# Rounding a weight slab at the end of a unit instead of after the chain steps that follow it

## The chip, the cores and the metric

The kernel runs on one core of a Trainium2 chip. A core has five engines that run side by side, each through its own list of instructions in order: PE (TensorE, matrix products), DVE (VectorE), ACT (ScalarE), POOL (GpSimd) and SP (SyncE, which here only issues DMAs). Engines wait for each other by semaphores. Matrix products land in PSUM, which has eight banks; everything else lies in SBUF. The metric is the device time of one execution in microseconds (us), lower is better; with more than one run the median is taken.

## The reference

The input `x` has 256 tokens of 1024 features, in fp32. It goes through two layers.

- **First block.** An adaLN modulation (`silu(c) @ ada_w`, giving shift, scale and gate) of an rms norm, one product with `w_in`, then two branches: an RWKV-7 scan of 8 heads, and attention of 8 heads over a latent of 128 features, in which an indexer scores all keys (`relu(qi . ki)`, weighted by `wi`), the 64 best keys of each query are kept, and a T5 bias is added. Each branch is multiplied by `silu(z)` and by its output matrix (`w_pa`, `w_pb`); the sum, gated by two sigmoids (`g_a`, `g_b`), goes through `w_o`, times the modulation's gate, back onto `x`; then an rms norm.
- **Second block.** A SwiGLU feed-forward part (2816 hidden features), a mixer of two branches (an HGRN2 scan and causal attention with forget gates, "fox"; each with its output matrix, gated, then `w_out`), cross attention to 256 memory tokens, and a second feed-forward part.

```python
br_a = (y_a * jax.nn.silu(z_a)) @ w_pa[l]
br_b = (y_b * jax.nn.silu(z_b)) @ w_pb[l]
merged = jax.nn.sigmoid(g_a) * br_a + jax.nn.sigmoid(g_b) * br_b
x = x + gate[:, None, :] * (merged @ w_o[l])
...
x = x + 0.5 * rmsnorm(swiglu(h, ffn1_w_in[l], ffn1_w_down[l]), ffn1_post_g[l])
```

All of the weights are fp32 and are read once, some 195 MB in all with what is written. The result has to be as precise as fp32 products.

## The kernel before

**Products in three passes.** PE's fast format, fp32r, has fewer bits than fp32. So every operand is split in two: a part rounded to fp32r, and the remainder. A product is three matmuls, hi x hi, hi x lo and lo x hi (`mm3`, L699 to L702). The left or right operand, an activation such as `hThi` and `hTlo`, is split once; the weights are split slab by slab as they come in.

**Slabs.** The weights come as 332 slabs, nearly all of 1024 elements in each of 128 partitions (512 KB). 324 of them are split. Each passes through this line:

1. SP loads it into one of four buffers `raw` (`slab_in`, L647 to L656). The load of slab i waits until slab i-4 is used up: its remainder made, or, if it is a slab that isn't split, PE past it.
2. ACT rounds it: `whi<-raw`, 128x1024, into one of three buffers (`round_slabs`, L1311 to L1321). It waits until the raw slab has landed, and until PE has used the slab three before in the ring (`use`).
3. POOL subtracts: `wlo<-raw,whi` (`remainders`, L2642 to L2656), in four pieces of 128x256, or in one piece in most of the feed-forward parts. It waits for the rounding.
4. PE waits for both (`weights`, L707) and runs the unit's matmuls.

The eight slabs of the modulation's gate (`ada_w`) are not split. PE reads them straight out of `raw` (`gate_unit`, L769; in the trace `ps<-raw,cs`). Two of them follow each of the four groups `g0` to `g3`, the products for the branch gates.

**The order.** Every engine walks the same list, made once in `Plan.lay_out` (L397 to L460) from a table of costs. Its entries are mainly *units*, a slab's product in two halves, and *steps* of *chains*: the serial parts, such as the RWKV heads (`head0`, `head1`), the attention of the first block (`dsa`), the HGRN scan (`hgrn`), the norm at a part's start. Each chain is a generator on each engine, and a step advances it on all of them. Steps stand where the planner thinks that their inputs are ready, between units or halves of units. An engine that has nothing to do in an entry passes on.

**ACT's own list.** ACT's loop (L1818 on) calls `unit(u, half)`. At half 0 it rounds ahead, up to the slab two behind the unit's own (`u.ahead` is three, in the first units two): the buffer for that one was used by the unit just before. At the last half it evacuates finished banks (`outs`, such as `gab`, the branch gates). Between these calls it does the chains' work: `rl` (L1645) copies the indexer's scores out of two banks, with the relu; `x<-ps` copies a head's output; `sq` and `mu` are a head's norm; `olT` (L1657) copies an attention head's output, from which PE makes `ps<-olT,wuv` two heads at a time (L1133); `oahi<-qb` is the rounded half of the fox output's split, and DVE makes its remainder `oalo<-qb,oahi`; `hi_` and `gt` are squares for the mixer's norms. `w2a` is the buffer that takes the modulation gate's sum.

**Banks.** Of the eight PSUM banks the units have three (0 to 2), and the chains five (3 to 7), in turn (`bank`, L693). The first matmul into a bank waits until the engine that had to empty it has done so.

Of the kernel before, what the change touches and what calls it, by code (L numbers as in the profile page):

```python
# [470 lines left out]
def program(nc, I, consts, vecs, out):  # L471
    with ExitStack() as ctx:
# [6 lines left out]
        slabs, place, order = plan.slabs, plan.place, plan.order  # L479
# [824 lines left out]
        def scalar(e):  # L1304
# [3 lines left out]
            def act(o, i, f, **k):  # L1308
                return e.activation(o, i, f, **k)  # L1309

            def round_slabs(upto):  # L1311

                while ahead[0] < min(upto, len(plan.split)):
                    c = ahead[0]
                    i = plan.split[c]
                    n = slabs[i][1][0] * slabs[i][1][1]
                    w.wait_ge(S["raw", i % NRAW], i)
                    if c >= NHL:
                        w.wait_ge(S["mm"], ("use", plan.split[c - NHL]))
                    act(whi[c % NHL][:, 0:n], raw[i % NRAW][:, 0:n], ACT.Copy).then_inc(S["hi"].tick(i), 1)  # L1320
                    ahead[0] += 1  # L1321
# [75 lines left out]
            def post(stage, t):  # L1397
                half = stage in ("f1", "f2")
                r = st[:, 12 + t:13 + t]
                for key in {"f1": [("d1", t, 0), ("d1", t, 1)], "f2": [("d2", t, 0), ("d2", t, 1)],  # L1400
                            "mix": [("wout0", t), ("wout1", t)], "mem": [("wmo0", t), ("wmo1", t)]}[stage]:
                    w.wait_ge(S["ev_a"], key)
                act(r, st[:, 8 + 2 * t:9 + 2 * t], ACT.Identity, bias=st[:, 9 + 2 * t:10 + 2 * t]).then_inc(S["post_a"].tick(), 1)
                w.wait_ge(S["post_a"])
                act(r, r, ACT.Sqrt, scale=(4.0 if half else 1.0) / 1024, bias=C("eps", 2 if half else 0, 1)).then_inc(
                    S["post_a"].tick((stage, t)), 1)
# [57 lines left out]
            def square_out(p, key, t, n):  # L1464
                w.wait_ge(S["ev_v"], key)
                act(p, p, ACT.Square, accum_out=st[:, 8 + 2 * t + n:9 + 2 * t + n]).then_inc(S["ev_a"].tick(key), 1)
# [23 lines left out]
            def unit(u, half):  # L1490
                if half == 0 and u.kind != "gate":
                    round_slabs(place[u.slab] + u.ahead)
                if u.kind == "tail" or (u.kind == "down" and u.last):
                    for n in (range(2) if u.kind == "down" else [half % 2]):
                        t = half if u.kind == "down" else half // 2
                        w.wait_ge(S["mm"], ("acc", u.grp, t, n))
                        square_out(PS[bank_of[u.grp, t, n]][:, :], (u.grp, t, n), t, n)
                        if n == 1:
                            post("f" + u.arg[0], t)
                elif u.last and u.ev in outs and u.kind != "down":  # L1500
                    if u.kind == "tm":
                        w.wait_ge(S["mm"], ("acc", u.grp, half))
                        outs[u.ev](u, half)
                    elif half == 1:
                        w.wait_ge(S["mm"], ("acc", u.grp))
                        outs[u.ev](u, half)

            def turn_over(tag, u):
                b = PS[bank_of["turn", tag, u]]
                w.wait_ge(S["turn_pe"], (tag, u))  # L1510
                act(FF[tag]["a"][0][:, 2 * u:2 * u + 2, :], b[:, :].rearrange("p (j t) -> p j t", j=2), ACT.Copy).then_inc(
                    S["turn_a"].tick((tag, u)), 1)
# [305 lines left out]
            for what, *d in order:  # L1818
                if what == "unit":
                    unit(*d)  # L1820
                elif what == "step":
                    if d[0] in chains:
# [862 lines left out]
        for count in (sync, tensor, vector, scalar, gpsimd):  # L2685
            count(Blank())
        for signal in S.values():
            signal.counted()
        with nc.Block() as block:
            block.sync(sync)  # L2690
            block.tensor(tensor)
            block.vector(vector)
            block.scalar(scalar)
            block.gpsimd(gpsimd)
# [34 lines left out]
```

## Time and profile before

| | us |
|---|---|
| median of 3 runs | 1231.42 |
| lowest and highest run | 1228.05, 1234.56 |
| the profiled execution | 1229.5 |
| its span (first to last instruction) | 1227.7 |

| engine | busy us | share | instructions |
|---|---|---|---|
| PE | 1155.5 | 94% | 8388 |
| POOL | 916.2 | 75% | 927 |
| ACT | 594.4 | 48% | 867 |
| DVE | 466.1 | 38% | 802 |

The mean clock that TensorE was granted is 0.989 of full speed. "Busy" counts each engine's own instructions, whoever waits for them; an engine can be busy for little of the time and still be what others wait for at a given place. The page also lists idle time before a group of instructions and what ended it. That idle time costs something only where the engine that waits is the one that others are waiting for.

### The profile page before, as it was taken

The numbers are of one execution on the slowest core, as the hardware profiler recorded it, in microseconds if no ns is written. First come the engines' busy times: TensorE is split into PE (matmuls) and PEld (weight loads), VectorE is DVE, ScalarE is ACT, GpSimd is POOL, SyncE is SP. The second block draws the span as 40 slices with busy tenths as digits, with TensorE's granted clock in tenths as the row PEclk, the third lists the DMA queues.
The fourth block names the chain that finished last, engine by engine and source line by source line (L and its number), as shares of the span: only waits on it lengthen the run. The fifth ranks groups of instructions, "written<-read, shape, count | busy, mean of one in ns | idle before, by whom it ended". The sixth has DMA issues, their size and how long they took to land.

```text
span 1227.7 us, 21194 instructions
## 1 busy us (share of the span) xinstructions
PE 1155.5 (94%) x8388; PEld 978.1 (80%) x8388; DVE 466.1 (38%) x802; ACT 594.4 (48%) x867; POOL 916.2 (75%) x927
## 2 busy tenths in 40 slices
PE   7999799999899999999999989999899989999997
PEld 7899798677687888788987876878677977888785
DVE  5527555654544111102435566433434133111101
ACT  6374432433656445435554545755345446445433
POOL 4689854531298888796899998678898857888794
PEclk9999999999999999999999999999999999999999
DMA  9887432333165656565565544354675525656562
GB/s 337 269 275 214 121 88 88 103 107 102 65 217 168 201 178 186 169 200 161 144 169 145 145 139 138 105 155 150 197 252 172 155 85 161 198 177 186 169 198 94
DMA packets 182899, 202.10 MB, mean 165 GB/s; under 512 B 7529, under 2 KB 141073, under 8 KB 182033
## 3 DMA queue, kind: packets, MB, share of 16 engines
q1 hardware_dynamic: 177584, 185.78, 50.8%
q10 hardware_dynamic: 5216, 14.97, 3.5%
q8 instruction: 67, 1.10, 0.4%
q14 instruction: 32, 0.25, 0.1%
HBM read 196.51 MB, written 4.21 MB: 163 GB/s over the span
## 4 chain that ended last, share of the span: by engine, by line
PE 67%; POOL 15%; issue 7%; DVE 6%; ACT 4%; POOLq 0%; DMA 0%; ACTq 0%; DVEq 0%
PE ps L700 19%; PE ps L702 18%; PE ps L701 17%; POOL wlo L2654 15%; PE ps L697 11%; PE ps L705 2%; ACT whi L1309 1%; DVE x L1882 1%; DVE oalo L1874 1%; ACT L1309 0%; DVE red L2327 0%; ACT rl L1309 0%; DVE tmp L1879 0%; DVE hE L1874 0%; DVE gt L1874 0%
## 5 line engine op out<-in xcount | busy, mean ns | idle before, releaser
L2654 POOL TENSOR_TENSOR wlo<-raw,whi 128x256 fp32r<-128x256 f32 (+1 forms) x918 | 910.7, 1026 | 294.7 <-ACT whi L1309 293.3
L1309 ACT ACTIVATE whi<-raw 128x1024 fp32r<-128x1024 f32 x324 | 340.3, 1056 | 297.4 <-PE ps L702 267.0
L700 PE MATMUL ps<-whi,hThi 128*128 128x512 f32 (+1 forms) x656 | 264.5, 403 | 14.4 <-POOL wlo L2654 8.9
L702 PE MATMUL ps<-whi,hTlo 128*128 128x512 f32 (+1 forms) x656 | 255.9, 390 | 0.0
L701 PE MATMUL ps<-wlo,hThi 128*128 128x512 f32 (+1 forms) x656 | 255.4, 389 | 0.0
L700 PE MATMUL ps<-hThi,whi 128*128 128x256 f32 x568 | 166.6, 293 | 13.5 <-issue 4.1
L701 PE MATMUL ps<-hTlo,whi 128*128 128x256 f32 x568 | 161.3, 284 | 0.0
L702 PE MATMUL ps<-hThi,wlo 128*128 128x256 f32 x568 | 161.1, 284 | 0.0
L700 PEld LDWEIGHTS ps<-whi,hThi 128*128 128x128 f32 x656 | 123.9, 189 | 46.5 <-issue 18.6
L702 PEld LDWEIGHTS ps<-whi,hTlo 128*128 128x128 f32 x656 | 124.0, 189 | 26.5
L701 PEld LDWEIGHTS ps<-wlo,hThi 128*128 128x128 f32 x656 | 124.2, 189 | 21.9
L700 PEld LDWEIGHTS ps<-hThi,whi 128*128 128x128 f32 x568 | 109.3, 192 | 21.0 <-issue 12.4
L701 PEld LDWEIGHTS ps<-hTlo,whi 128*128 128x128 f32 x568 | 109.5, 193 | 0.1
L702 PEld LDWEIGHTS ps<-hThi,wlo 128*128 128x128 f32 x568 | 109.3, 193 | 0.0
L700 PE MATMUL ps<-whi,aThi 128*128 128x512 f32 x176 | 69.1, 392 | 2.6 <-POOL wlo L2654 2.3
L701 PE MATMUL ps<-wlo,aThi 128*128 128x512 f32 x176 | 68.5, 389 | 0.0
L702 PE MATMUL ps<-whi,aTlo 128*128 128x512 f32 x176 | 68.5, 389 | 0.0
L1874 DVE TENSOR_TENSOR aTlo<-ps,aThi 128x512 fp32r<-128x512 f32 x22 | 15.2, 692 | 111.9 <-ACT aThi L1309 111.9
L1882 DVE SCALAR_TENSOR_TENSOR ac<-ps,st,sg 128x256 f32<-128x256 f32 x44 | 21.1, 484 | 92.5 <-ACT sg L1309 92.5
L700 PE MATMUL ps<-whi,oahi 128*128 128x512 f32 x128 | 52.7, 411 | 3.8 <-DVE oalo L1874 3.1
L1309 ACT ACT_TABLE_LOAD x39 | 50.0, 1283 | 6.5 <-DVE gt L1874 2.6
L701 PE MATMUL ps<-wlo,oahi 128*128 128x512 f32 x128 | 50.7, 396 | 0.0
(386 smaller groups left out, 1538.7 us busy)
## 6 DMA issues: line engine op xcount, KB each, us to landing
raw<-in_w_in SPq DMA_DIRECT2D x120, 512.0 KB, 3.6
raw<-in_ffn_w_in SPq DMA_DIRECT2D x176, 256.0 KB, 3.1
raw<-in_ffn_w_down SPq DMA_DIRECT2D x44, 512.0 KB, 4.2
raw<-in_w_mkv SPq DMA_DIRECT2D x16, 512.0 KB, 6.4
raw<-in_ada_w SPq DMA_DIRECT2D x8, 512.0 KB, 5.6
raw<-in_w_o SPq DMA_DIRECT2D x8, 512.0 KB, 4.3
raw<-in_w_branch_a SPq DMA_DIRECT2D x8, 512.0 KB, 3.7
raw<-in_w_branch_b SPq DMA_DIRECT2D x8, 512.0 KB, 3.7
```

The source lines that it names most:

```text
L697: return e.matmul(o, l, r, start=start, stop=stop)
L700: e.matmul(o, l[0], r[0], start=start, stop=False)
L701: e.matmul(o, l[0], r[1], start=False, stop=False)
L702: return e.matmul(o, l[1], r[0], start=False, stop=stop)
L705: return e.transpose(b[:, o:o + 128], src, ident)
L1309: return e.activation(o, i, f, **k)
L1874: return e.tensor_tensor(o, a, b, op)
L1882: return e.scalar_tensor_tensor(out=o, in0=a, scalar=s, in1=b, op0=op0, op1=op1)
L2654: p = e.tensor_tensor(wlo[c % NHL][:, o], raw[i % NRAW][:, o], whi[c % NHL][:, o], ALU.subtract)
```

## The change

At the end of a unit's second half, behind the evacuation of its banks, ACT now rounds one slab more than it has at this place before: the one three behind the unit's own, whose buffer this very unit has used. Before, this rounding was issued at the start of the next unit, behind all chain steps, table loads, copies and DMA issues that stand between the two. The modulation gate's units, the last ones (`tail`) and the memory keys' (`key`) are left as they are. No instruction is added or removed; on PE, DVE, POOL and SP the order is the same.

```diff
@@ -1504,6 +1504,8 @@
                     elif half == 1:
                         w.wait_ge(S["mm"], ("acc", u.grp))
                         outs[u.ev](u, half)
+                if half == 1 and u.kind not in ("gate", "tail") and u.ev != "key":
+                    round_slabs(place[u.slab] + 1 + u.ahead)
 
             def turn_over(tag, u):
                 b = PS[bank_of["turn", tag, u]]
```

**ACT at the branch gates.** ACT's rows behind the last bank of group `g0` at about 219 us, before. `gab` evacuates the gates' bank, `whi0<-raw3` is the rounding of the third slab of group `g1`.

```order
L1309 ACTIVATE gab<-ps2 128x512
L1309 ACTIVATE rl<-ps7 128x512
L1309 ACTIVATE rl<-ps3 128x512
L1309 ACTIVATE x<-ps4 128x64
L1309 ACTIVATE x<-ps5 128x64
L1309 ACTIVATE sq<-x 128x256
L1309 ACTIVATE x<-ps7 128x64
L1309 ACTIVATE x<-ps3 128x64
L1309 ACT_TABLE_LOAD
L1309 ACTIVATE mu<-mu,con 128x4
L1309 ACTIVATE sq<-x 128x256
L1309 ACTIVATE w2a2<-ps0 128x256
```

The rounding is the next row behind these. The same place after the change:

```order
L1309 ACTIVATE gab<-ps2 128x512
L1309 ACTIVATE whi0<-raw3 128x1024
L1309 ACTIVATE rl<-ps7 128x512
L1309 ACTIVATE rl<-ps3 128x512
L1309 ACTIVATE x<-ps4 128x64
L1309 ACTIVATE x<-ps5 128x64
L1309 ACTIVATE sq<-x 128x256
```

The rounding has moved ahead of eleven rows, the two `rl` copies first. PE's rows at that place, which the change leaves as they are (`raw3,cs` is the modulation gate's slab, in the same buffer `raw3` that the rounding above will read once it is loaded anew; `XU`, `TB`, `TK` belong to a head):

```order
L697 MATMUL ps6<-XU,WT 64x64
L697 MATMUL ps6<-XU,WG 64x64
L697 MATMUL ps0<-raw3,cs 32x256 x4
L697 MATMUL ps7<-XU,TB 64x64 [waits s_ds_a,s_h1_v]
L697 MATMUL ps7<-XU,TB 64x64
L697 MATMUL ps7<-VT,TK 64x64 x2
L697 MATMUL ps3<-XU,TB 64x64 x2
```

The wait for `s_ds_a` in the fourth row is the one for ACT's `rl` copies out of banks 7 and 3.

**ACT at the end of the attention branch**, at about 329 us, before; `whi0<-raw1` is the rounding of the third slab of `w_pa`.

```order
L1309 ACT_TABLE_LOAD
L1309 ACTIVATE gab<-ps1 128x512
L1309 ACTIVATE gab<-ps2 128x512
L1309 ACTIVATE olT<-ps4 128x256
L1309 ACTIVATE w2a2<-ps0 128x256
L1309 ACTIVATE olT<-ps7 128x256
L1309 ACTIVATE whi0<-raw1 128x1024
L1309 ACTIVATE olT<-ps3 128x256
```

And after:

```order
L1309 ACT_TABLE_LOAD
L1309 ACTIVATE gab<-ps1 128x512
L1309 ACTIVATE gab<-ps2 128x512
L1309 ACTIVATE whi0<-raw1 128x1024
L1309 ACTIVATE olT<-ps4 128x256
L1309 ACTIVATE w2a2<-ps0 128x256
L1309 ACTIVATE olT<-ps7 128x256
L1309 ACTIVATE olT<-ps3 128x256
```

Two `olT` copies and a `w2a` copy now stand behind the rounding.

**ACT at the fox output's split**, at about 869 us, before:

```order
L1309 ACTIVATE whi1<-raw1 128x1024
L1309 ACTIVATE oahi<-qb 128x512
L1309 ACTIVATE whi2<-raw2 128x1024
L1309 ACTIVATE oahi<-qb 128x512
L1309 ACTIVATE whi0<-raw3 128x1024
L1309 ACTIVATE oahi<-qb 128x512 x2
```

And after:

```order
L1309 ACTIVATE whi1<-raw1 128x1024
L1309 ACTIVATE whi2<-raw2 128x1024
L1309 ACTIVATE oahi<-qb 128x512
L1309 ACTIVATE whi0<-raw3 128x1024
L1309 ACTIVATE oahi<-qb 128x512
L1309 ACTIVATE whi1<-raw0 128x1024
L1309 ACTIVATE oahi<-qb 128x512 x2
```

Each copy comes one rounding later, and the rounding of `raw0`, which stood behind a DMA issue after the last copy, is now ahead of the last two.

## Rows read from the trace of the kernel before

**Rows 1.** The page: busy time, and two groups of instructions (columns as headed).

```profile
span 1227.7 us, 21194 instructions
...
PE 1155.5 (94%) x8388; PEld 978.1 (80%) x8388; DVE 466.1 (38%) x802; ACT 594.4 (48%) x867; POOL 916.2 (75%) x927
...
## 5 line engine op out<-in xcount | busy, mean ns | idle before, releaser
L2654 POOL TENSOR_TENSOR wlo<-raw,whi 128x256 fp32r<-128x256 f32 (+1 forms) x918 | 910.7, 1026 | 294.7 <-ACT whi L1309 293.3
L1309 ACT ACTIVATE whi<-raw 128x1024 fp32r<-128x1024 f32 x324 | 340.3, 1056 | 297.4 <-PE ps L702 267.0
```

**Rows 2.** The page: the chain that ended last, by engine.

```profile
PE 67%; POOL 15%; issue 7%; DVE 6%; ACT 4%; POOLq 0%; DMA 0%; ACTq 0%; DVEq 0%
```

**Rows 3.** Waits, whole span: us in total, times, longest.

```profile
PE ps L700 <- POOL wlo L2654: 17.4, 17, 2.4
```

**Rows 4.** Waits of PE from 150 to 1212 us.

```profile
PE ps L700 <- POOL wlo L2654: 10.0, 12, 2.4
```

**Rows 5.** Timeline, ACT, 218 to 229 us: start, us, instruction, idle before.

```profile
221.17 1.08 ACT L1309 ACTIVATE rl<-ps 128x512 f32<-128x512 f32 x2 [2.01 <-PE ps L697]
...
228.77 1.05 ACT L1309 ACTIVATE whi<-raw 128x1024 fp32r<-128x1024 f32 x1
```

**Rows 6.** Timeline, SP's issues and ACT's rounding, 223 to 237 us.

```profile
223.51 0.37 SPq L656 DMA_DIRECT2D raw<-in_w_in  x1
...
233.15 0.37 SPq L656 DMA_DIRECT2D raw<-in_w_in  x1
...
236.78 1.06 ACT L1309 ACTIVATE whi<-raw 128x1024 fp32r<-128x1024 f32 x1 [3.58 <-DMA raw<-in_w_in]
```

**Rows 7.** Timeline, PE, 222 to 234 us.

```profile
222.81 0.64 PE L697 MATMUL ps<-raw,cs 128*32 128x256 f32 x8
223.38 0.34 PE L697 MATMUL ps<-XU,TB 128*64 128x64 f32 x4
...
233.27 0.47 PE L700 MATMUL ps<-whi,hThi 128*128 128x512 f32 x1 [2.43 <-POOL wlo L2654]
```

**Rows 8.** Windows: busy time by engine, granted clock, DMA share, GB/s.

```profile
core 0: us, PE busy (x) PEld busy (x) DVE busy (x) ACT busy (x) POOL busy (x), PEclk, DMA share, GB/s
233.20:238.00 4.80, 4.73 (x16) 3.22 (x17) 3.02 (x9) 1.06 (x2) 2.95 (x5) 0.64 0.53 141
...
650.00:750.00 100.00, 91.05 (x1274) 80.16 (x1260) 63.65 (x79) 47.09 (x51) 95.93 (x107) 1.00 0.53 142
880.00:888.00 8.00, 7.28 (x24) 5.60 (x24) 3.58 (x6) 2.08 (x2) 2.85 (x6) 0.79 0.66 216
```

**Rows 9.** Timeline, ACT and PE, 330 to 336 us.

```profile
330.42 0.39 ACT L1309 ACTIVATE olT<-ps 128x256 f32<-128x256 f32 x1
331.06 0.38 ACT L1309 ACTIVATE w2a<-ps 128x256 f32<-128x256 f32 x1 [0.26 <-PE ps L697]
331.88 0.38 ACT L1309 ACTIVATE olT<-ps 128x256 f32<-128x256 f32 x1 [0.44 <-PE ps L697]
334.31 1.06 ACT L1309 ACTIVATE whi<-raw 128x1024 fp32r<-128x1024 f32 x1 [2.04 <-DMA raw<-in_w_pa]
...
333.82 0.65 PE L697 MATMUL ps<-olT,wuv 128*64 128x256 f32 x4
```

**Rows 10.** Timeline, ACT: start of the mixer (576, 586), memory output (1002).

```profile
576.25 1.04 ACT L1309 ACTIVATE hi_<-x 128x1024 f32<-128x1024 f32 x1
...
586.79 2.01 ACT L1309 ACTIVATE whi<-raw 128x1024 fp32r<-128x1024 f32 x2
...
1002.48 1.99 ACT L1309 ACTIVATE whi<-raw 128x1024 fp32r<-128x1024 f32 x2
```

**Rows 11.** Timeline, DVE, POOL and PE, 865 to 885 us.

```profile
870.98 10.20 DVE L1874 TENSOR_TENSOR oalo<-qb,oahi 128x512 fp32r<-128x512 f32 x2 [3.74 <-ACT oahi L1309]
...
882.30 1.28 DVE L1874 TENSOR_TENSOR oalo<-qb,oahi 128x512 fp32r<-128x512 f32 x2
...
865.41 14.62 POOL L2654 TENSOR_TENSOR wlo<-raw,whi 128x256 fp32r<-128x256 f32 x21
...
880.72 0.47 PE L700 MATMUL ps<-whi,oahi 128*128 128x512 f32 x1 [3.06 <-DVE oalo L1874]
```

**Rows 12.** Groups of POOL's instructions, 650 to 750 us.

```profile
L2654 POOL TENSOR_TENSOR wlo<-raw,whi 128x256 fp32r<-128x256 f32 x107 | 96.6, 940 | 4.1 <-ACT whi L1309 4.0
```

## The prediction

> **What bounds the kernel now.** I read the page from the top, then the waits over the whole span, then the places where the change moves something, each in time order. The page shows TensorE (PE) busy 94% of the span, GpSimd (POOL) 75%, ScalarE (ACT) 48% [rows 1]; the chain of waits gives PE 67%, POOL 15%, ACT 4% [rows 2]. So PE sets the time, and POOL where it is late with a remainder `wlo`. POOL waits for ACT's rounded slab `whi` 293.3 us in all [rows 1], but that costs only where PE waits too: PE waits for `wlo` 17.4 us in 17 places [rows 3], of which 10.0 us in 12 places lie behind 150 us [rows 4]. The first number is the reader's trap: almost all of it is slack. An ACT queue that is half idle is not harmless either. ACT runs its list in order, so what a rounding waits for, everything behind it waits for as well. The question is thus not whether ACT has the time, but what stands behind each moved rounding, and whether that rounding can start.
>
> A rounding needs two things: the buffer used three slabs before, which the change waits for at just the right moment, and the raw slab landed. SP loads raw slab i only when slab i-4 is used up (L647-656). Normally that slab's remainder is done long before. Not so at the adaLN gate: its slabs go unsplit into PE (`ps<-raw,cs`), and the load four slabs on waits for PE to pass them.
>
> **Part 1, the branch-gate group at 220 us.** Before, the rounding starts at 228.77, behind eleven short instructions, the first of them the two copies `rl` at 221.17 [rows 5]. Now it stands ahead of `rl`. Its raw slab is issued by SP at 223.51, straight after PE's gate matmuls of 222.81 to 223.45 [rows 6, 7]. Issue to landing I read from a rounding that waited for nothing else: issued 233.15, rounding 236.78, so 3.6 us [rows 6]. The rounding then runs from 227.2 to 228.3 (1.06 us, [rows 1]) and both `rl` copies (1.08 us, [rows 5]) end at 229.4. PE's next row behind the gate matmuls, `ps<-XU,TB`, writes the bank that `rl` empties; it started at 223.38 [rows 7] and now can't before 229.4: PE loses 6.1 us. That it isn't a deadlock is because the gate matmuls stand just ahead of that row. Given back is the wait of 2.43 us for the slab's remainder at 233.27 [rows 7], since that slab is now rounded 0.5 us earlier and PE comes later. After that stall PE was granted 0.64 of its clock from 233.2 to 238 [rows 8], which costs 4.8 x 0.36 = 1.7 us; the new stall, longer, will bring the same a little earlier, so I count no difference. The norm chain behind `rl` slips some 7 us, but PE's next row for it (239) slips 3.7 too and had room. Sum: **+3.7**, bounds +1 (if the load lands sooner and the chain has room) and +6.
>
> **Part 2, the end of the attention branch at 330 us.** The same trap. The rounding that waited for its DMA until 334.31 [rows 9] is now ahead of two `olT` copies of 330.42 and 331.88 and one `w2a` copy. It still starts at 334.31, so they run from 335.37: 0.39, 0.38 and 0.38 us [rows 9] end at 336.5. PE's `ps<-olT,wuv`, which needs both heads' copies, was at 333.82 [rows 9]: **+2.7** of PE, nothing given back, since PE waited for no slab there. PE's clock may fall for it: a stall of 2.43 us brought the 0.64 above. So 0 to +1.7 more, and I take half, +0.8. The other two gate groups move only a `w2a` copy that nobody waits for soon.
>
> **Part 3, chain instructions one rounding late.** Where a chain is what PE waits for, an ACT instruction of it now stands behind a rounding that can run, and comes 1.06 us later: the first square of the mixer's norm at 576.25 [rows 10], the softmax at 811, the second square at the mixer's end at 939, and half of it at the decay exponentials at 127. That is 3.5 x 1.06 = 3.7, by the rounding's own time [rows 1]. The two FFN starts, where squares and the last `hThi` copies slip by 1 to 2 us, cost about 0.5 each. Sum **+4.7**, bounds +1 and +6. The twenty `aThi` copies in the FFNs come about half a rounding later, 0.55 us; PE waits for none of them now and I count nothing.
>
> **Part 4, slabs that come sooner.** The rounding of 586.79 goes to 576.4 and the one of 1002.48 to 988.6 [rows 10]; similar at 94, 390, 515, 654, 908 and 1160. These end stalls of PE: 1.4 us at 587, 1.0 at 394, 0.4 at 98, 0.2 at each FFN's down start. Where POOL is the limit, the lead stays: 650 to 750, with POOL 95.93 of 100 us and PE 91.05 [rows 8], and the last slabs ahead of 940 and of 1023. There I take how much sooner POOL starts: 1.4 at 655, 1.4 at 909, 2.0 at 1003. Sum **-8.1**; it can't be much over the 10.0 - 2.4 = 7.6 of PE's own waits plus those lags, so bounds -4 and -10.
>
> **Part 5, the output split at 871 us.** VectorE's `oalo<-qb,oahi` and its neighbour take 10.20 us from 870.98, though two such at 882.30 take 1.28; POOL works without a gap from 865.41 to 880.03, and PE waits 3.06 us until 880.72 [rows 11] and then runs at 0.79 of its clock until 888 [rows 8]. So this VectorE instruction, two operands from SBUF, was shut out until POOL paused. Now the four `oahi` copies come behind roundings, some 3 us later, and POOL gets one slab more (the one rounded at 884.04 before) before it pauses, at 882.9. If VectorE is shut out again, PE starts near 883.7 instead of 880.72, but with two slabs of lead: +1.4. If it gets in between two pieces, as nearly all its instructions in 650 to 750 do (POOL's 107 pieces there have a mean of 940 ns, [rows 12], against 14.62 / 21 = 0.70 us in the run without VectorE, [rows 11]), the stall, its clock loss and the slab's lateness go: -4.5 to -5. A shut-out as long as this is there once in the trace, so I take **-4.5** as the likelier, and +1.4 as its other bound.
>
> The Trainium skill ("SBUF — State Buffer", "SBUF: two separate sides") says that VectorE with two SBUF inputs and GpSimd take a shared port pair as an exclusive lock, for a whole instruction, and the other blocks. The row of 10.20 us agrees in kind; that a loser can lose 12 pieces in a row is not in the rule. By the rule alone one wait is at most one piece, and the sum would be -4.5.
>
> **The sum.** +3.7 + 2.7 + 0.8 + 4.7 - 8.1 - 4.5 = -0.7, on the profiled execution's 1229.5 us (span 1227.7 [rows 1] and 1.8 around it): 1228.8. The median of the runs shown, 1231.42, is 1.9 above that execution: 1230.7, rounded to **1231**, no change.
>
> **Rivals.** (a) *Faster*: the waits for raw slabs don't reach PE, because another bank is taken or the slab lands earlier. For it: ACT is 52% idle. Against it: the two roundings that waited for their DMA [rows 6, 9], and PE's bank row right behind the gate. Then part 1 is -2.4 and part 2 nothing: -0.7 - 6.1 - 2.7 - 0.8 = -10.3, so 1221. (b) *Slower*, one mechanism: PE is stopped at 871 until POOL pauses, as before and later than before, because earlier roundings make POOL's run longer by one slab. Part 5 turns to +1.4, which is 5.9 worse: +5.2. It also holds elsewhere, wherever POOL is fed without a gap: part 4 then loses up to half, +4. Together +5 to +9, so about 1238. It decides once part 4 gives under 7 us. For it: the row of 10.20 us, and a POOL run that is made longer. Against it: in 650 to 750 VectorE got in within a piece or two each time. (c) *Nothing moves*: roundings are off the path everywhere, and ACT's order doesn't matter; 1231. Against it: PE's 10.0 us of waits for `wlo`, and part 1.
>
> **Chances.** Forecast 0.46, (a) 0.22, (b) 0.25, (c) 0.07. About 0.5%, 6 us, is what a measurement of this kernel can tell from no change. Forecast and (c) lie within it: 0.53. Faster 0.22, slower 0.25. The likeliest case alone: 1226 to 1236 from the bounds of parts 1 to 4 taken together. The range that leaves out 2 in 10 goes to 1224 on the side of (a), and to 1239 on that of (b).
>
> **What the profile of the changed kernel would show.** Part 1: the rounding of this slab waiting for `DMA raw` until about 227, `rl` copies at 228 to 229, an idle stretch of PE of about 6 us from 223.4, and no wait for `wlo` on that slab. Part 2: `olT` copies right behind a rounding that waited for DMA, and PE idle 2.7 us ahead of `ps<-olT,wuv`. Part 3: the first `hi_` square at 577.4, counted from the same place. Part 4: PE's waits for `wlo` behind 150 us down from 10.0 to 3 us or less. Part 5: an `oalo` of about 1 us, and no wait of PE in front of `ps<-whi,oahi`. I am wrong if the `rl` copies come before the rounding or PE has work it can do in between, if PE's waits for `wlo` stay, or if `oalo` again takes as long as POOL runs.

## The result, and the profile after

| | before | changed |
|---|---|---|
| median (lowest, highest), us, side by side on one chip | 1232.99 (1228.05, 1243.14) | 1246.05 (1245.67, 1250.05) |
| ratio to before, 95% interval | | 1.013 (1.0092 to 1.0169) |
| later, with the last experiments | 1230.75 | 1248.17 |
| the profiled execution, us | 1229.5 | 1250.05 |
| its span, us | 1227.7 | 1248.2 |

The change makes the kernel slower by some 13 to 17 us, 1.3 to 1.4%. The forecast was 1231, and slower had a chance of 0.25. The page of the changed kernel:

```profile
span 1248.2 us, 21196 instructions
...
PE 1164.4 (93%) x8388; PEld 988.0 (79%) x8388; DVE 472.9 (38%) x802; ACT 596.1 (48%) x867; POOL 921.1 (74%) x927
...
PE 67%; POOL 12%; DVE 7%; ACT 6%; issue 4%; DMA 3%; POOLq 0%; ACTq 0%; DVEq 0%
```

Against [rows 1] PE is busy 8.9 us longer with the same 8388 matmuls: that is a lower clock, not a wait. Of the 20.5 us of span, the other 11.6 are idle time of PE. In the chain [rows 2] POOL has fallen from 15% to 12%, and DMA, which had none, has 3%. PE's waits over the whole span, largest first (us in total, times, longest):

```profile
PE ps L700 <- POOL wlo L2656: 12.2, 12, 2.0
PE ps L697 <- DVE XU L1887: 7.3, 2, 6.9
PE ps L697 <- DVE hE L1876: 6.2, 6, 1.7
PE ps L700 <- DVE oalo L1876: 5.8, 1, 5.8
...
PE ps L705 <- ACT gt L1309: 3.6, 2, 3.1
...
PE ps L697 <- ACT olT L1309: 2.9, 1, 2.9
...
PE ps L705 <- DVE gab L1876: 1.5, 1, 1.5
```

The first row was 17.4 us in 17 places [rows 3]: earlier slabs did take waits away. The `XU` row is the gate group at 220 us (part 1), `oalo` the output split (part 5), `olT` the end of the attention branch (part 2), `gt` the mixer's end (part 3), `gab` the output of the first block's branches at 374 us, which the prediction doesn't name. The row before the change for the same place at the mixer's end, beside an `ACT gt` of 0.5 us:

```profile
PE ps L705 <- DVE gt L1878: 2.4, 1, 2.4
```

So of the 3.6 us of waits there, 2.9 were there before.

**Where it is lost.** The slabs that are split have the numbers 0 to 323, in order. PE's matmuls have the same order in every trace, so I read, in both traces, when PE starts on a given slab. What the difference between two slabs grows by is what the stretch between them costs. The last two columns part it into PE's idle time and its busy time; with the same matmuls, more busy time is mainly a lower clock.

| from slab to slab | place in the program | us | of it idle | busy |
|---|---|---|---|---|
| start of the span to 38 | first block's products | -1.7 | -1.5 | -0.2 |
| 38 to 46 | gate groups g0 and g1 (part 1) | +4.8 | +4.5 | +0.3 |
| 46 to 49 | g1, g2: PE waits 0.73 and 1.05 us for head steps | +2.0 | +1.8 | +0.2 |
| 49 to 55 | g2, g3; no new stall | +4.1 | -0.7 | +4.7 |
| 55 to 60 | attention branch's end (part 2) | +4.5 | +2.9 | +1.7 |
| 60 to 64 | first block's output; PE waits 1.47 us for `gab`, see part 3 | +1.7 | +1.5 | +0.2 |
| 64 to 76 | first FFN's start | +0.8 | +0.8 | 0.0 |
| 76 to 210 | first FFN, mixer | -3.4 | -1.1 | -2.3 |
| 210 to 225 | fox output's split (part 5) | +3.5 | +2.7 | +0.9 |
| 225 to 246 | mixer's end (part 3) | +3.1 | +1.0 | +2.2 |
| 246 to 320 | memory, second FFN | -0.5 | -0.1 | -0.4 |
| 320 to the end | last slabs | +1.6 | 0.0 | +1.6 |

**The gate group at 220 us**, as the timelines of ACT and PE and SP's issues of the changed kernel have it:

```profile
225.42 1.06 ACT L1309 ACTIVATE whi<-raw 128x1024 fp32r<-128x1024 f32 x1 [7.92 <-DMA raw<-in_w_in]
226.38 1.07 ACT L1309 ACTIVATE rl<-ps 128x512 f32<-128x512 f32 x2
```

```profile
226.99 1.43 DVE L1884 SCALAR_TENSOR_TENSOR sc<-rl,wi,sc 128x256 f32<-128x256 f32 x2 [8.05 <-ACT rl L1309]
228.34 0.28 DVE L1887 COPY XU<-ps 128x128 f32<-128x128 f32 x1
```

```profile
221.15 0.64 PE L697 MATMUL ps<-raw,cs 128*32 128x256 f32 x8
228.67 0.48 PE L697 MATMUL ps<-XU,TB 128*64 128x64 f32 x4 [6.89 <-DVE XU L1887]
```

```profile
221.85 9.81 SPq L656 DMA_DIRECT2D raw<-in_w_in  x2
```

PE passes the modulation gate's slab by 221.8, SP issues the load at 221.85, the rounding waits until 225.42 and both `rl` copies come behind it: step by step what the prediction says. One link more than I counted shows: VectorE, in order too, uses `rl` before it copies `XU`, so PE waits for that copy (its end is 228.34 + 0.28 = 228.62), 1.2 us behind the last `rl`. Before, the same matmuls followed the gate's directly [rows 7]. The windows from PE's stall on, first the stall, then what follows it:

```profile
221.80:228.70 6.90, 0.03 (x2) 0.03 (x2) 1.67 (x4) 2.25 (x5) 2.15 (x3) 0.59 0.27 76
228.70:234.00 5.30, 5.30 (x40) 3.74 (x41) 4.02 (x11) 2.22 (x5) 0.99 (x2) 0.57 0.30 69
```

PE then works for 5.3 us at 0.57 of its clock, mostly at the lower of its two levels, which costs 5.3 x 0.43 = 2.3 us.

**The attention branch's end**, ACT and then PE:

```profile
344.03 1.06 ACT L1309 ACTIVATE whi<-raw 128x1024 fp32r<-128x1024 f32 x1 [5.24 <-DMA raw<-in_w_pa]
344.99 0.36 ACT L1309 ACTIVATE olT<-ps 128x256 f32<-128x256 f32 x1
345.26 0.38 ACT L1309 ACTIVATE w2a<-ps 128x256 f32<-128x256 f32 x1
345.52 0.39 ACT L1309 ACTIVATE olT<-ps 128x256 f32<-128x256 f32 x1
```

```profile
345.96 1.12 PE L697 MATMUL ps<-olT,wuv 128*64 128x256 f32 x4 [2.86 <-ACT olT L1309]
```

A wait of 2.86 us where 2.7 was predicted.

**The output split.** DVE and POOL of the changed kernel:

```profile
886.61 10.11 DVE L1876 TENSOR_TENSOR oalo<-qb,oahi 128x512 fp32r<-128x512 f32 x2 [6.55 <-ACT oahi L1309]
...
897.84 1.28 DVE L1876 TENSOR_TENSOR oalo<-qb,oahi 128x512 fp32r<-128x512 f32 x2
```

```profile
857.48 38.09 POOL L2656 TENSOR_TENSOR wlo<-raw,whi 128x256 fp32r<-128x256 f32 x52 [1.14 <-ACT whi L1309]
```

The first `oalo` alone takes 9.50 of the 10.11 us, from 886.61 to 896.1; POOL's run of 52 pieces without a gap ends at 857.48 + 38.09 = 895.57. Compare [rows 11], where POOL's run ends at 880.03 and `oalo` with it. VectorE was shut out again, from a start that comes 2.8 us later in the program's time, to the end of a run that is longer by one slab. PE's idle time ahead of this slab is 5.79 us, where it was 3.06.

### The profile page after: what moved, and what is told of

Its sections match the earlier page's. It is cut to its first block, busy times and chain, and to the rows that moved or that the text cites. A ratio compares the mean times of both kernels' runs of the same rounds, so it can differ in the third digit from the quotient of the medians.

```text
span 1248.2 us, 21196 instructions
## 1 busy us (share of the span) xinstructions
PE 1164.4 (93%) x8388; PEld 988.0 (79%) x8388; DVE 472.9 (38%) x802; ACT 596.1 (48%) x867; POOL 921.1 (74%) x927
## 4 chain that ended last, share of the span: by engine, by line
PE 67%; POOL 12%; DVE 7%; ACT 6%; issue 4%; DMA 3%; POOLq 0%; ACTq 0%; DVEq 0%
PE ps L700 18%; PE ps L702 18%; PE ps L701 18%; POOL wlo L2656 12%; PE ps L697 11%; PE ps L705 2%; ACT whi L1309 2%; DMA raw<-in_w_in 1%; DVE x L1884 1%; DVE oalo L1876 1%; DMA raw<-in_w_o 1%; DMA raw<-in_w_out 1%; ACT L1309 1%; ACT yg L1309 0%; ACT st L1309 0%
## 5 line engine op out<-in xcount | busy, mean ns | idle before, releaser
L700 PEld LDWEIGHTS ps<-hThi,whi 128*128 128x128 f32 x568 | 109.8, 193 | 16.3 <-issue 11.2
L702 PE MATMUL ps<-whi,oalo 128*128 128x512 f32 x128 | 51.5, 403 | 0.0
```

The source lines that it names most:

```text
L700: e.matmul(o, l[0], r[0], start=start, stop=False)
L702: return e.matmul(o, l[1], r[0], start=False, stop=stop)
```

## Experiments

A unit has the number of its own slab among the split ones, and rounds early the slab three on. An experiment on the change narrows the condition in its added `if` by this number, `p = place[u.slab]`. The units meant are: 42, the last of `g0` (part 1); 54, the last of `g3` (part 2); 215 to 217, the three ahead of the output split (part 5).

**Which places cost.** All but the two gate units; the two alone; all but the three at fox; ten units that the first trace made look useful.

```
e1_all_but_two:  ... and p not in (42, 54)
e2_only_two:     ... and p in (42, 54)
e3_not_at_fox:   ... and p not in (215, 216, 217)
e4_ten_units:    ... and p in (16, 71, 114, 136, 157, 159, 184, 225, 249, 301)
```

> The change, without the early rounding at two units: the last unit of g0 and the last of g3. There the rounding stands ahead of chain copies and its raw slab is still behind the modulation gate's slab on PE. Theory A (these two round trips PE -> SP -> DMA -> ACT -> PE cost 4.7 and 4.4 us in the profile of the changed kernel, and the PE clock falls behind them costs more): 10 to 14 us faster than the changed kernel, so 1232 to 1236, and within 4 us of before. Rival B (the loss is spread over all chain steps that now stand behind a rounding): 3 us or less faster than the changed kernel, so 1243 or more.

> The kernel before, with the early rounding at those two units alone. Theory A: 9 to 13 us slower than before. Rival B: at most 5 us slower.

> The change, without the early rounding at the three units ahead of the fox output's split (the copies oahi stand again where they stood before). If later oahi copies and one more POOL slab are what made the wait there grow from 3.1 to 5.8 us, with its clock loss: 3 to 4 us faster than the changed kernel, oalo starts at the same distance from its unit as before and is still shut out for some 9 us. If VectorE's shut-out is chance: no difference, or a shut-out in another place.

> The kernel before, with the early rounding at ten units alone: those behind which the rounding started late and PE or a full POOL waited for the remainder (slabs 19, 74, 117, 139, 160, 162, 187, 228, 252 and 304 of those that are split). Theory A (early roundings help where the raw slab is there and POOL is late): 4 to 8 us faster than before. Rival B (chain instructions behind a rounding cost as much as the lead brings): within 2 us of before.

| | median (range), us | ratio to before, interval |
|---|---|---|
| before, beside them | 1230.46 | |
| e1_all_but_two | 1239.28 (1233.28 to 1247.4) | 1.0056 (1.0029 to 1.0083) |
| e2_only_two | 1243.46 (1234.44 to 1248.27) | 1.0075 (1.0045 to 1.0105) |
| e3_not_at_fox | 1242.91 (1238.51 to 1244.1) | 1.0084 (1.0052 to 1.0116) |
| e4_ten_units | 1230.33 (1224.03 to 1237.48) | 0.9988 (0.9961 to 1.0016) |

Before itself ranges from 1224.9 to 1243.0 beside these, and the ratio lies in places 3 us below the quotient of the medians (e2: 0.75% is 9.2 us, the medians 13.0), so I read single medians to some 3 us. Two roundings, moved alone, cost 9 to 13 us, most of the loss. The page and the waits of `e2_only_two`:

```profile
span 1244.0 us, 21194 instructions
...
PE 1164.9 (94%) x8388; PEld 985.1 (79%) x8388; DVE 466.2 (37%) x802; ACT 594.9 (48%) x867; POOL 915.7 (74%) x927
```

```profile
PE ps L697 <- DVE XU L1887: 7.4, 2, 7.0
```

It has the one long stall of part 1 (+5.6 us from slab 38 to 49, all of it up to 46) and of part 2 (+2.4 from 55 to 64). Those are 8 us; its span is 16.3 longer. The other 8 us or so are PE's clock (busy 1164.9 against 1155.5 [rows 1]), and lie where it orders nothing differently: 1.5 between slabs 49 and 55, 2.7 between 225 and 246, 2.9 between 246 and 250, 1.6 behind 320. Without the two, `e1_all_but_two` has no jump between slabs 38 and 46 (the 2.0 us from 46 to 49 stay) and is 6.8 us below the change, 8.8 above before: less than theory A asked for (10 to 14, within 4 of before) and more than rival B allowed. So the places are settled, not the whole loss. That alone they seem worth more than their absence saves fits the clock: taken out at the 0.76 us per us found below, both ways come to some 6 us in the means, an estimate.

Without the three at fox, `e3_not_at_fox` is 3.1 us below the change, as expected, and its `oalo` is shut out as in before (9.58 us). So the early roundings don't cause the shut-out; they only make it end later.

`e4_ten_units` is no change at all, where earlier slabs were to give some us. Its trace gains 3.6 us from slab 137 to 163, but loses 5.7 from slab 74 to 76:

```profile
401.56 0.77 PE L700 MATMUL ps<-whi,hThi 128*128 128x512 f32 x1 [3.35 <-POOL wlo L2656]
```

I had kept unit 71's early rounding and left out unit 72's. Unit 71's waits for PE with the norm's last copies and its four squares behind it, and the rounding after them comes 2.1 us later than in before. With unit 72's moved as well (e1) PE waits 0.7 us there. A rounding's place acts on its neighbours: units 71 and 72 are one decision.

**Is it the shut-out, and does POOL's pause end it?** POOL is made to wait for the copies that VectorE is to make, ahead of three slabs' remainders; nothing else changes. The keys are those of `oalo`'s pieces and of the norm step behind the mixer and the memory part.

```
in remainders, behind the wait for "use":
+                    for s_, key in PAUSE.get(c, ()):
+                        w.wait_ge(S[s_], key)
e5_pool_pauses:         before, PAUSE at slabs 217, 218, 220 (oalo)
e6_pool_pauses_change:  the change, PAUSE at 218, 219, 220 (oalo)
e7_pool_pauses_3:       e5, and at 236, 259 (the x of mixer and memory)
e8_eight_and_pauses:    e5's and 259, and early roundings where
                        p in (16, 114, 136, 157, 159, 184, 249, 301)
```

> The kernel before, with POOL waiting for VectorE's oalo pieces (one ahead of each of two slabs, the last ahead of a third), so that it can't run through. Theory C (VectorE's instruction is shut out for as long as POOL has pieces ready, whatever their number): oalo takes about 0.7 us, PE's wait of 3.1 us ahead of the fox output's product goes and the clock loss behind it too, 3 to 5 us faster than before. Rival D (oalo waits for something else, so that POOL's pause changes nothing): oalo is again at 9 us or starts later, no gain.

> The changed kernel with the same pauses of POOL, each one slab later, as the oahi copies are. Theory C: PE's wait of 5.8 us goes, 5 to 8 us faster than the changed kernel, so 1238 to 1241. Rival D: no gain.

> As the first of these, and POOL also waits for VectorE's two additions to x at the mixer's end and at the memory part's end, where an instruction was shut out for 4.4 and 2.4 us. Theory C: each then takes about 1.3 us; the memory part's chain is 1.1 us shorter, the mixer's about 2 us shorter, but PE's slab there comes 2.7 us later: 4 to 6 us faster than before in all.

> The early rounding at eight units alone (the ten without the one at the first FFN's start, where the next rounding came late, and without the one at w_out, which brought nothing), with POOL's pauses for oalo and at the memory part's end. At an equal PE clock 3 us from the roundings, 4 from the pauses, 1 from the memory part: 6 to 9 us faster than before. If whatever is gained is lost again in PE's clock: 3 us or less.

| | median (range), us | ratio to before, interval |
|---|---|---|
| before, beside them | 1230.04 | |
| e5_pool_pauses | 1229.0 (1226.24 to 1233.31) | 0.9985 (0.9964 to 1.0006) |
| e6_pool_pauses_change | 1240.32 (1235.6 to 1247.01) | 1.0075 (1.0045 to 1.0105) |
| e7_pool_pauses_3 | 1227.92 (1223.92 to 1229.92) | 0.9972 (0.9952 to 0.9991) |
| e8_eight_and_pauses | 1223.87 (1221.81 to 1224.66) | 0.9936 (0.9914 to 0.9957) |

DVE and POOL of `e5_pool_pauses`:

```profile
873.33 1.32 DVE L1875 TENSOR_TENSOR oalo<-qb,oahi 128x512 fp32r<-128x512 f32 x1 [3.73 <-ACT oahi L1310]
876.18 0.69 DVE L1875 TENSOR_TENSOR oalo<-qb,oahi 128x512 fp32r<-128x512 f32 x1 [1.53 <-ACT oahi L1310]
```

```profile
854.48 19.62 POOL L2657 TENSOR_TENSOR wlo<-raw,whi 128x256 fp32r<-128x256 f32 x28
874.81 9.79 POOL L2657 TENSOR_TENSOR wlo<-raw,whi 128x256 fp32r<-128x256 f32 x12 [0.72 <-DVE oalo L1875]
```

A pause of POOL of 0.72 us turns 9.5 us of VectorE into 1.32: the shut-out, and what ends it, are shown. PE gains 2.4 us there (from +2.37 at slab 216 to -0.06 at 219). By the median it is 1 us, within the noise, where I expected 3 to 5. In the change the like pauses are worth more: 6.4 us in the trace (from slab 216 to 219 the changed kernel falls back 3.9 us on before, e6 gains 2.4), 5.7 by the medians (1240.32 against 1246.05). The pause at 236 takes the mixer's `x<-gt` from 4.40 to 1.64 us but holds POOL up, and PE gains nothing there; `e7_pool_pauses_3` is 2.1 us below before, not 4 to 6.

`e8_eight_and_pauses` is the best of all, 6.2 us below before; each of its ten executions is below the lowest of before's 106 beside the experiments (1224.9). It keeps eight early roundings at starts of parts, and the pauses:

```profile
span 1220.9 us, 21194 instructions
...
PE 1152.2 (94%) x8388; PEld 977.7 (80%) x8388; DVE 460.7 (38%) x802; ACT 595.6 (49%) x867; POOL 921.1 (75%) x927
```

Its lead grows where part 4 put it: 1.6 us at slab 139 (the mixer's start), 3.5 by slab 157, 6.6 behind the output split, 6.8 at the end.

**One place at a time, on top of the best.**

```
e9_most_and_pauses:  the change with e8's pauses, and p not in
                     (42, 54, 72, 192, 193, 197, 215, 216, 217, 235, 257, 258, 259)
e10_one_late_raw:    e8, and 42
e11_fox_early:       e8, and 215, 216, 217, without the pauses at oalo
```

> The change at all units but thirteen: without the two whose raw slab is late, the three at the fox output's split, and eight at the starts of the first and second FFN, in the softmax and norm at 790 to 830 us and at the mixer's end, where a chain instruction stands behind the rounding; with POOL's pauses for oalo and at the memory part's end. If the loss of the change is in these places: as good as the version with eight early roundings, 1222 to 1226. If being behind a rounding costs in many more places (a rounding is 1.06 us, and some thirty more are moved): 1228 or more.

> The version with eight early roundings and the pauses, and the early rounding behind the last unit of g0 on top: one round trip through the modulation gate's slab. The stall itself costs 4.5 us (6.9 added, 2.4 given back). If the PE clock falls more often or longer for it, 7 us or more are lost to that version, and the mean granted clock is lower by 0.002 or more; if the clock follows chance alone, 4 to 5 us and the same clock.

> The version with eight early roundings, with the three at the fox output's split added and without POOL's pauses for oalo: part 5 by itself. Theory C: oalo is shut out until POOL has made the remainder of one slab more, PE waits 5.8 us there: 5 to 7 us slower than the version with eight roundings. If VectorE now gets in (what I had forecast): about as fast.

| | median (range), us | ratio to before, interval |
|---|---|---|
| before, beside them | 1229.3 | |
| e9_most_and_pauses | 1228.54 (1223.86 to 1230.55) | 0.9988 (0.9973 to 1.0003) |
| e10_one_late_raw | 1228.06 (1224.27 to 1237.71) | 0.9993 (0.9969 to 1.0016) |
| e11_fox_early | 1226.14 (1223.04 to 1235.79) | 0.9985 (0.9962 to 1.0009) |

One rounding moved, at 42: +4.2 us against e8 by the median, +5.5 in the trace from slab 38 to 49, of which 4.5 are idle time of PE. Its mean clock is 0.984 against e8's 0.986, so the outcome lies between the two that I had set: the stall is most of it, and the clock takes some. ACT and PE's window behind the stall in `e10_one_late_raw`:

```profile
226.19 1.06 ACT L1310 ACTIVATE whi<-raw 128x1024 fp32r<-128x1024 f32 x1 [7.95 <-DMA raw<-in_w_in]
227.15 1.07 ACT L1310 ACTIVATE rl<-ps 128x512 f32<-128x512 f32 x2
```

```profile
229.00:236.00 7.00, 6.56 (x42) 4.71 (x43) 5.65 (x17) 2.91 (x7) 1.46 (x2) 0.52 0.38 96
```

`e11_fox_early` has part 5 as the change has it, DVE and then PE:

```profile
869.93 10.14 DVE L1877 TENSOR_TENSOR oalo<-qb,oahi 128x512 fp32r<-128x512 f32 x2 [6.56 <-ACT oahi L1310]
```

```profile
879.62 0.76 PE L701 MATMUL ps<-whi,oahi 128*128 128x512 f32 x1 [5.84 <-DVE oalo L1877]
```

From slab 216 to 219 it falls back 4.0 us on before and 6.4 on e8, and ends 3.9 behind e8; by the median only 2.3, where I expected 5 to 7. (The ratios to before, 0.9985 and 0.9936, are 6 us apart: its executions spread from 1223 to 1236.) `e9_most_and_pauses` shows that early roundings in most units bring no more than the eight: it repeats e4's stall at slab 75 (3.3 us), since unit 72 is left out there as well.

**What is left of the change without its costly places, and the change again.**

```
e12_without_five:  ... and p not in (42, 54, 215, 216, 217)
e13_change_again:  the change, unaltered
```

> The change without its early rounding in the two gate units (places 42 and 54) and in the three at the fox stage (215 to 217); every other unit rounds early as in the change. Theory: these five places cause the whole loss, the rest gives back a few us by earlier slabs: 1226 to 1234, no jump of the PE starts at slabs 46, 56 and 219, and the end within 4 us of before at equal clock. Rival: the rest costs too, by the lower TensorE clock behind many small stalls (mean clock about 0.980, as with all but the two, 1239.28 us at 0.9804): then 1236 to 1242. Together with all but the two (1239.28) and not at fox (1242.91), the sum of the single savings (6.8 and 3.1 us off 1246.05) would put it at 1236.

> The change itself, once more, for more executions of it beside its variants: 1243 to 1248 us, mean TensorE clock 0.977 to 0.981. If the clock of the four executions so far was ill luck, the median comes down to about 1240 with a clock near 0.984; if the clock is part of the price of the change, it stays.

| | median (range), us | ratio to before, interval |
|---|---|---|
| before, beside them | 1230.75 (1227.25 to 1236.22) | |
| e12_without_five | 1233.26 (1229.22 to 1244.21) | 1.0027 (1.0005 to 1.0048) |
| e13_change_again | 1248.17 (1245.8 to 1248.82) | 1.0144 (1.0126 to 1.0163) |

Five places make 14.9 of the 17.4 us here; all the other moved roundings together cost 2.5. The rival, by which they would cost 5 to 11 us through the clock, is not borne out. The trace of `e12_without_five` has no jump between slabs 38 and 44 (0.0 us), is 1.6 us behind at 210 and 4.5 behind at 246. The 2.9 us between lie at the mixer's end, PE:

```profile
943.53 1.97 PE L705 MATMUL ps<-con,gt 128*128 128x128 f32 x8 [3.10 <-ACT gt L1309]
```

That is the second square behind the rounding of unit 235 (part 3). But only 0.7 us of it is new: before, PE waited 2.4 us for VectorE ahead of the same matmuls. The rest is clock, PE being busy 2.1 us longer for the same matmuls. And it isn't this rounding's doing alone: `e2_only_two`, which moves nothing here, has the wait of before,

```profile
PE ps L705 <- DVE gt L1880: 2.4, 1, 2.4
```

and yet loses 2.7 us in the same stretch, all of it clock.

## Why the prediction was wrong

Term by term, the forecast against the profiled pair (parts by PE's idle time, the clock by its busy time):

| term | forecast, us | measured, us |
|---|---|---|
| part 1 | +3.7 | +4.5 |
| part 2, its stall | +2.7 | +2.9 |
| parts 3 and 4 | +4.7 - 8.1 = -3.4 | +1.6 |
| part 5 | -4.5 (with its clock) | +2.7 |
| clock | +0.8 | +8.9 |
| sum (terms rounded) | -0.7 | +20.5 |

Three terms failed: part 5, the clock, and the sum of parts 3 and 4.

**Part 1: right.** Predicted +3.7 (a stall of 6.1 less 2.4 given back; the rows it was worked out from give 5.9). The stall is 6.9, longer by VectorE's `sc` ahead of its `XU`. From slab 38 to 46 the trace shows +4.8, e2 +5.6, e10 +5.5, of which 4.5 are idle time each time. The rest is the clock: I counted no difference, since before had a dip there too [rows 8]. But that one cost 1.7 us at 0.64 and these cost 2.3 (the window above) to 3.4 us (7.0 x 0.48 in e10).

**Part 2: right.** +2.7 predicted; stall 2.86, e2 +2.3. The +0.8 for the clock was 1.7 in this execution (slab 55 to 60) and 0.1 in e2.

**Parts 3 and 4: right in kind, the sum too good by 5 us.** The terms of part 4 come to 8.0, not 8.1; that is nothing beside what was left out of part 3. Two waits behind chains that I didn't name are new, 1.8 us between slabs 46 and 49 and 1.5 between 60 and 64. They stand in each of the seven traces in which these units round early (1.0 to 2.4 and 0.4 to 1.5 us) and in none of the others. The second is the trap of parts 1 and 2 once more, on a slab of `w_o`, without the modulation gate in it; ACT, DVE and PE of the changed kernel:

```profile
370.97 1.06 ACT L1309 ACTIVATE whi<-raw 128x1024 fp32r<-128x1024 f32 x1 [3.12 <-DMA raw<-in_w_o]
371.94 0.57 ACT L1309 ACTIVATE hThi<-ps 128x512 fp32r<-128x512 f32 x1
```

```profile
372.55 0.69 DVE L1876 TENSOR_TENSOR hTlo<-ps,hThi 128x512 fp32r<-128x512 f32 x1 [3.97 <-ACT hThi L1309]
373.88 0.69 DVE L1876 TENSOR_TENSOR gab<-ps,gab 128x512 f32<-128x512 f32 x1
```

```profile
374.62 0.66 PE L705 MATMUL ps<-con,gab 128*128 128x128 f32 x4 [1.47 <-DVE gab L1876]
```

ACT waits for the slab, the chain's copy `hThi` behind it is late, VectorE's `hTlo` and `gab` with it, and PE waits for `gab`. In the first, too, ACT waits for a raw slab ahead of a copy of the chain (2.24 us, at 243.46), but I haven't followed it from there to PE's waits. Where I had counted 1.06, at the mixer's end, the stall grew by 0.7, and the clock took 2 us more. e12, which has these parts and none of the others, is 2.5 above before by the median; e8, with a pick of part 4 and a pause at 259, is 5.1 below e5. So the picked gains are worth some 5 us, not 8.1, and what the other moves cost comes to some 7, not 4.7. PE's waits for `wlo` behind 150 us fell from 10.0 [rows 4] to 4.5 us in 6 places, and not to 3 or less.

**Part 5 failed, by the mechanism and not only the size.** I wrote that a shut-out as long as this is there once in the trace, and took -4.5 as the likelier, with VectorE getting in between two pieces. It was +3.5 in the profiled execution, 8 us worse, and 3.1 by medians (e3). And -4.5 was too much even for a VectorE that gets in: e5 shows -2.4. The comparison behind it was false. POOL's mean of 940 ns in 650 to 750 [rows 12] averages over VectorE's other instructions; that some get in says nothing on this one. (`hE<-hE,hq` 128x512, with two operands like `oalo`, takes 1.23 us at 677.54 in the trace of before, in the middle of a gapless run of POOL, and 0.68 alone: it waited less than one piece.) Three instructions are shut out in every trace in which POOL isn't made to pause for them, and with the same length: `oalo` 9.49 to 9.62 us, the mixer's `x<-gt` 4.37 to 4.43, memory's `x<-kb` 2.38 to 2.40. In the changed kernel, DVE:

```profile
947.28 4.41 DVE L1884 SCALAR_TENSOR_TENSOR x<-gt,st,x 128x1024 f32<-128x1024 f32 x1
951.79 1.28 DVE L1884 SCALAR_TENSOR_TENSOR x<-gt,st,x 128x1024 f32<-128x1024 f32 x1
...
1043.14 2.38 DVE L1884 SCALAR_TENSOR_TENSOR x<-kb,st,x 128x1024 f32<-128x1024 f32 x1
```

Like instructions with and without the long wait stood in the trace of before; I had looked at one. The Trainium skill ("SBUF — State Buffer", "SBUF: two separate sides") states that whichever engine starts first gets the shared port pair for its whole instruction while the other blocks. That the loser then gets the next turn, "at most one piece", was my own step from it, and it doesn't hold for this row: the loser waited 9.5 us, some 13 pieces long, in each of the eight kernels that don't pause POOL for it. The measurement decides. This was rival (b)'s mechanism, at this one place. Its price was set too low for a lack of the clock: a stall of 5.8 us, and then

```profile
896.20:904.00 7.80, 7.74 (x22) 6.13 (x23) 2.92 (x5) 1.06 (x1) 1.05 (x2) 0.61 0.62 202
```

which costs 7.8 x 0.39 = 3.0 us where before's row at 0.79 costs 8 x 0.21 = 1.7 [rows 8].

**The clock failed too.** I allowed +0.8 for it, at one place. The changed kernel's nine executions have a mean clock of 0.978, none of them above 0.980; those of before (106, beside the experiments) have 0.986, six of them 0.980 or less. Within each kernel of this study the time rises by 0.76 us per us of 1228 that the clock takes: 0.0075 x 1228 x 0.76 = 7 us of the 16 to 18 between the medians. In the profiled pair it is the 8.9 us of PE's busy time. The stretches with the three new stalls hold 2.9 of it, net of before's own dips (0.3, 1.7 and 0.9). The rest lies where the change brings PE little or no new wait: 4.7 from slab 49 to 55, 2.2 at the mixer's end, 1.6 behind slab 320, less 2.3 from 76 to 210. The stretch from slab 49 to 55 costs +4.1 us in the profiled execution. The same program run again (e13) has +0.8 there. The changed kernel's window first, then e13's at the same matmuls:

```profile
294.00:302.00 8.00, 8.00 (x61) 6.60 (x60) 2.43 (x7) 0.38 (x1) 1.44 (x3) 0.57 0.23 70
```

```profile
297.00:305.00 8.00, 8.00 (x93) 6.42 (x94) 3.15 (x9) 1.71 (x3) 3.00 (x6) 1.00 0.22 69
```

In both, PE had just waited 1.5 us (1.49 and 1.48) for a chain; once the clock fell behind it, once not. So where the clock falls is partly drawn anew in each execution. That the mean stays low in all nine is the change's doing; through which of its waits isn't settled.

By medians, then: the two gate places 7 (taken out, e1) to 13 (alone, e2), the output split 3 (e3) to 6 (e12 against e1), the remaining roundings 2.5, each with its clock; by e12 the first two together are 15.

The three rivals: (a) and (c) are out. (b) had part 5's mechanism right and gave 1238, 8 us short. The output split is 3 to 6 of the loss; the gate places, which (b) priced like the forecast, and the clock, which it didn't price, are more of it.

## What to carry to other kernels

A load, or any work, that is put ahead on an in-order engine must be able to run when its turn comes: look at what its buffer waits for (here a slab that PE reads itself, or a load that is simply not there yet), then at the first thing behind it, on that engine and on the next. Most such moves are worth a microsecond or two in either direction; two out of some three hundred made about half of the loss or more here, so choose them one by one, and neighbours together. A shut-out of one engine by another seen once is to be expected again at the same instruction, and a short pause of the other engine ends it, though here that brought 6 us in the changed kernel and only 1 us, within the noise, in the one before. To a new stall of TensorE of 6 to 7 us add 2 to 3 us for the clock behind it; behind one of 2 to 3 us it was 0.1 in one trace and 1.7 in another. Part a stretch's loss into idle and busy time of the engine that bounds it before you call it a stall or the clock: at the mixer's end 3.1 us of wait were 0.7 new.

## What the runs showed of the hardware

- A VectorE instruction with two operands from SBUF that takes 0.68 us alone took 9.49 to 9.62 us behind GpSimd's gapless run of 128x256 pieces, and ended within 0.6 us of that run's end; with a pause of 0.72 us it took 1.32. Two others took 4.37 to 4.43 and 2.38 to 2.40 us instead of 1.28, in every trace without a pause for them. Others got in between pieces (a `hE<-hE,hq` took 1.23 us, 0.68 alone). What tells them apart isn't known.
- After a stall of 5.8 to 7.0 us TensorE was granted 0.50 to 0.61 of its clock for 5 to 8 us. A stall of 1.5 us was followed by 0.57 for 8 us in one execution and by the full clock in another of the same program. Behind the 2.4 us at the mixer's end, ahead of the same matmuls, it was 0.50 for 5.4 us in e2 and the full clock in before.
- The mean clock of one and the same program (before, 106 executions) ranged from 0.979 to 0.990, its time from 1224.9 to 1243.0 us.
